# Residuals written over the raw weight piece: 8 raw slots and 4 high buffers in place of 6, 3 and 3

## The chip, the cores and the metric

The kernel runs on one core of a Trainium2 chip. The metric is the device time of one execution in microseconds (us). Engine names are those of the profile: PE (matrix products), ACT (scalar engine), DVE (vector engine), POOL (GpSimd), SP (the engine that issues most transfers). SPq, ACTq are their DMA-issuing instructions. PEclk is the share of TensorE's full clock that was granted.

## What is computed

Two transformer blocks on 256 tokens of width 1024, in float32. Cut to what matters here:

```
# first block
proj = rmsnorm(x) @ w_in                      # 1024 x 3584
x = x + concat(stick_breaking(...), group_norm(retention(...)) * silu(r_g)) @ w_out
hn = rmsnorm(x); x = x + moe(hn)              # router, top 4 of 32 experts, 1024x2048 and 1024x1024 each
x = x + (p @ w_ple_proj) * sigmoid(rmsnorm(x) @ w_ple_gate)
# second block
q, k, v, z, xbc, dt, gates = split(rmsnorm(x) @ w_in_2)
attn = gqa_attention(rope(norm(q)), rope(norm(k)), v) @ w_attn_proj_2
ssd = ssd_branch(z, silu(conv(xbc)), dt) @ w_ssd_proj_2
x = x + rmsnorm((g_attn * attn + g_ssd * ssd) @ w_out_2)
x = x + rmsnorm((silu(gate) * up) @ w_down_2)  # gate, up = rmsnorm(x) @ w_gate_up_2
```

## The kernel before

**Pieces.** All weights but the experts' are cut into 89 pieces of at most 128 x 2048 floats (1 MB), numbered in the order of use: 0 to 13 `w_in`, 14 to 17 `w_out`, 18 router, then the experts, then the late pieces 19 to 22 `ple_gate`, 23 `ple_proj`, 24 and 25 `q`, 26 `kv`, 27 `dt`, 28 to 33 `xbc`, 34 to 41 `gates`, 42 to 45 `z`, 46 and 47 `attn_proj`, 48 to 51 `ssd_proj`, 52 to 55 `out2`, 56 to 77 the feed-forward's `gate` and `up`, 78 to 88 its `ffn_down`.

**A piece's way.** SP loads it into a raw slot (L380). ACT copies it, rounded, into a high buffer (`split`, L1058, 1.9 us), when the piece has landed and the high buffer's previous piece was used. POOL subtracts the high part from the raw piece and writes the residual (L1888, four instructions a piece). PE makes each product as three matmuls: high by high, high by low, low by high (L467 to L469), and counts `w_used` up. A product waits for `w_low`, the count of finished POOL pieces.

**The ring** has 12 slots of 2048 columns. In the dense parts 6 hold raw pieces (piece n in slot n % 6), 3 high parts, 3 low parts. A raw slot may be loaded again once POOL has finished its piece (`w_low`). In the expert phase all 12 slots hold one chunk each of an expert's weights: 8 `up` chunks, 4 `down` chunks; `EXPERT_SLOT` gives chunk j its slot.

**Order.** Every engine runs a list written out by hand and waits in it. SP: x, pieces 0 to 2, positions and 14 small broadcasts, the first pieces up to `RAW`, then the constants (`consts_late`, 1.9 MB, L394), then the rest. ACT: `split_to(n)` makes all splits up to piece n at that place of its list; between them stand its evacuations of PSUM, exponentials and the first half of each norm. In most places the call is `split_to(x + 3)`, followed by a wait until PE has used piece x and by the evacuation of x. After the experts ACT first splits `BUF` late pieces, then begins the norm (L1062, L1072) of the ple part. DVE does norms, rotations, softmax maxima, the convolution and the SSD weights. POOL has the residuals alone. Before the late pieces POOL waits until all experts are done.

```
def load(key):
    n = number[key]
    if n >= RAW:
        sp.wait_ge(sem("w_low"), n - RAW + 1)
    fetch(key)
...
    if m >= BUF:
        act.wait_ge(sem("w_used"), place[keys[m - BUF]] + 1)
    split(m)
```

Of the kernel before, what the change touches and what calls it, by code (L numbers as in the profile page):

```python
# [13 lines left out]
F32 = mybir.dt.float32  # L14
# [25 lines left out]
EPS = 1e-6  # L40
SLOT = 2048
RING = 12
RAW = 6
BUF = 3
EXPERT_SLOT = (1, 2, 3, 4, 5, 0, 6, 7, 8, 9, 10, 11)
PER_EXPERT = 12
CONVK = 5
CC = 12
# [77 lines left out]
def build_program(nc, a, out):  # L126
# [5 lines left out]
    pieces, number = [], {}  # L132
# [17 lines left out]
    before_experts = len(pieces)  # L150
    ROUNDS = E + (PASSES - 1) * E
    base_c = before_experts + PER_EXPERT * ROUNDS
    late = len(pieces)
# [20 lines left out]
    place = {k: n if n < late else n - late + base_c for k, n in number.items()}  # L174
    keys = sorted(number, key=number.get)

    def raw_slot(key):
        return number[key] % RAW

# [6 lines left out]
    def slot_fills(s):  # L186

        return sum(1 for k in keys if number[k] < late and raw_slot(k) == s) if s < RAW else 0

    with ExitStack() as ctx:  # L190
# [5 lines left out]
        def sem(name):  # L196
            return sems[name]
# [29 lines left out]
        arena_byte, ring_byte = nc.lookup_mloc(arena).addr, nc.lookup_mloc(ring).addr  # L227
# [17 lines left out]
        def parts_at(name, byte, cols):  # L245

            return nc.alloc_sbuf_tensor_at(name, [P, cols], F32R, offset=byte)[:, :]
# [70 lines left out]


        HIGH = [parts_at(f"w_high{i}", ring_byte + 4 * SLOT * (RAW + i), SLOT) for i in range(BUF)]  # L320
        LOW = [parts_at(f"w_low{i}", ring_byte + 4 * SLOT * (RAW + BUF + i), SLOT) for i in range(BUF)]

        def slot(s):
            return ring[:, s * SLOT:(s + 1) * SLOT]
# [5 lines left out]
        def split_view(key):  # L330

            _, chunks, width = pieces[number[key]]
            return [x[number[key] % BUF][:, 0:chunks * width].rearrange("p (k n) -> p k n", k=chunks) for x in (HIGH, LOW)]

        def chain(eng, name):

# [33 lines left out]
        def _(sp):  # L370
            def load(key):
                n = number[key]
                if n >= RAW:
                    sp.wait_ge(sem("w_low"), n - RAW + 1)
                fetch(key)

            def fetch(key):
# [11 lines left out]
            for at, name in GAINS:  # L389
                n = a[name].shape[1]  # L390
# [7 lines left out]
            def expert_load(e, j):  # L398
                dst = slot(EXPERT_SLOT[j])
                if j < KC:  # L400
# [11 lines left out]

            for j, s in enumerate(EXPERT_SLOT):
                if s < RAW:
                    sp.wait_ge(sem("w_low"), max(n for n in range(late) if n % RAW == s) + 1)
                else:
                    sp.wait_ge(sem("w_used"), before_experts)
                expert_load(0, j)
# [25 lines left out]
            with sp.Else():  # L444
                for j, s in enumerate(EXPERT_SLOT):

# [582 lines left out]
        def _(act):  # L1029
# [16 lines left out]
            def split_to(n):  # L1046

                while done_splits[0] <= min(n, len(keys) - 1):
                    m = done_splits[0]
# [3 lines that stand above are left out]
# [826 lines left out]
        @block.gpsimd  # L1879
        def _(pool):  # L1880
            for m, key in enumerate(keys):
                if m == late:
                    pool.wait_ge(sem("w_used"), before_experts + PER_EXPERT * ROUNDS)
                pool.wait_ge(sem("w_high"), m + 1)
                quarter = size(key) // 4
                for part in range(4):
                    at = slice(part * quarter, (part + 1) * quarter)
                    ins = nc.gpsimd.tensor_tensor(LOW[m % BUF][:, at], slot(raw_slot(key))[:, at], HIGH[m % BUF][:, at].bitcast(F32),  # L1888
                                                  ALU.subtract)
                ins.then_inc(sem("w_low"), 1)  # L1890

# [26 lines left out]
```

## Time and profile before

| | us |
|---|---|
| median of 3 runs | 1757.93 (1756.92 to 1758.99) |
| the profiled execution | 1748.9 |
| its span, first to last instruction | 1747.1 |
| busy: PE, DVE, ACT, POOL | 1498.8, 510.3, 423.6, 472.6 |

The profiled execution was 9.0 us shorter than the median of the runs. Parts by time, as the timeline shows them: input products, stick-breaking and retention until 208 us, router until 239, experts until 1189, ple until 1245, input products of the second block until 1301, attention until 1400, SSD until 1468, output products until 1545, feed-forward until the end.

### The profile page before, as it was taken

The numbers are of one execution on the slowest core, as the hardware profiler recorded it, in microseconds if no ns is written. First come the engines' busy times: TensorE is split into PE (matmuls) and PEld (weight loads), VectorE is DVE, ScalarE is ACT, GpSimd is POOL, SyncE is SP. The second block draws the span as 40 slices with busy tenths as digits, with TensorE's granted clock in tenths as the row PEclk, the third lists the DMA queues.
The fourth block names the chain that finished last, engine by engine and source line by source line (L and its number), as shares of the span: only waits on it lengthen the run. The fifth ranks groups of instructions, "written<-read, shape, count | busy, mean of one in ns | idle before, by whom it ended". The sixth has DMA issues, their size and how long they took to land.

```text
span 1747.1 us, 19158 instructions
## 1 busy us (share of the span) xinstructions
PE 1498.8 (86%) x7437; PEld 848.9 (49%) x7438; DVE 510.3 (29%) x826; ACT 423.6 (24%) x503; POOL 472.6 (27%) x360
## 2 busy tenths in 40 slices
PE   6787689999888888989888888987876988989997
PEld 5565443333232332323232332325675766779986
DVE  1766611211121111111121111112396168231211
ACT  4553300110010101001010101004442734343332
POOL 5862100000000000000000000005592643668894
PEclk9988879999999999999999999999997999999999
DMA  8522459999999999999999999996452322445540
GB/s 297 178 76 73 155 238 416 418 415 419 416 417 417 416 418 416 417 416 418 416 417 417 416 418 416 418 415 232 132 182 64 121 82 68 148 145 180 182 169 24
DMA packets 135830, 502.32 MB, mean 288 GB/s; under 512 B 11948, under 2 KB 42148, under 8 KB 102852
## 3 DMA queue, kind: packets, MB, share of 16 engines
q1 hardware_dynamic: 134480, 499.00, 72.9%
q10 hardware_dynamic: 1267, 2.09, 0.4%
q8 instruction: 67, 1.10, 0.3%
q14 instruction: 16, 0.12, 0.0%
HBM read 500.01 MB, written 1.05 MB: 287 GB/s over the span
## 4 chain that ended last, share of the span: by engine, by line
PE 41%; DMA 21%; SPq 16%; DVE 14%; issue 4%; ACT 3%; POOL 0%; ACTq 0%; DVEq 0%
DMA ring<-in_w_up_gate 19%; SPq L405 14%; PE PS L467 7%; PE PS L716 7%; PE PS L468 7%; PE PS L469 7%; PE PS L734 6%; ACT w_high L1058 1%; DMA ring<-in_w_ple_gate 1%; SPq L380 1%; PE PS L688 1%; DMA cst<-consts 1%; DVE arena L1605 1%; DVE arena L1608 1%; DVE arena L1603 1%
## 5 line engine op out<-in xcount | busy, mean ns | idle before, releaser
L1888 POOL TENSOR_TENSOR w_low<-ring,w_high 128x512 fp32r<-128x512 f32 (+1 forms) x356 | 472.4, 1360 | 1254.4 <-PEq L817 1006.9
L716 PE MATMUL PS<-ring,arena 128*64 128x512 f32 x2048 | 475.0, 604 | 53.9 <-DMA ring<-in_w_up_gate 53.8
L716 PEld LDWEIGHTS PS<-ring,arena 128*64 128x64 f32 x2048 | 134.4, 137 | 378.2 <-issue 214.5
L734 PE MATMUL PS<-ring,arena 128*64 128x512 f32 x1024 | 226.8, 594 | 23.5 <-issue 23.5
L1058 ACT ACTIVATE w_high<-ring 128x2048 fp32r<-128x2048 f32 (+1 forms) x89 | 167.4, 1882 | 275.1 <-PE PS L469 252.8
L1168 ACT ACTIVATE arena<-arena 128x512 f32<-128x512 f32 x32 | 20.1, 630 | 811.2 <-DVE arena L1602 811.2
L1602 DVE TENSOR_SCALAR arena<-PS 128x512 f32<-128x512 f32 x32 | 22.1, 692 | 514.0 <-PE PS L716 514.0
L467 PE MATMUL PS<-w_high,XNT_h 128*128 128x512 f32 (+1 forms) x336 | 137.5, 409 | 21.6 <-DVE XNT_l L1345 8.6
L734 PEld LDWEIGHTS PS<-ring,arena 128*64 128x64 f32 x1024 | 84.6, 137 | 145.1 <-issue 145.1
L467 PE MATMUL PS<-XNT_h,w_high 128*128 128x256 f32 (+1 forms) x464 | 131.2, 283 | 4.1 <-DVE XNT_l L1345 3.5
L468 PE MATMUL PS<-w_low,XNT_h 128*128 128x512 f32 (+1 forms) x336 | 133.6, 398 | 0.0
L469 PE MATMUL PS<-w_high,XNT_l 128*128 128x512 f32 (+1 forms) x336 | 133.5, 397 | 0.0
L468 PE MATMUL PS<-XNT_l,w_high 128*128 128x256 f32 (+1 forms) x464 | 131.7, 284 | 0.0
L469 PE MATMUL PS<-XNT_h,w_low 128*128 128x256 f32 (+1 forms) x464 | 131.6, 284 | 0.0
L1611 DVE COPY arena<-PS 128x512 f32<-128x512 f32 x32 | 22.1, 692 | 266.2 <-PE PS L734 266.2
L467 PEld LDWEIGHTS PS<-XNT_h,w_high 128*128 128x128 f32 (+1 forms) x464 | 87.0, 188 | 5.5 <-issue 4.2
L469 PEld LDWEIGHTS PS<-XNT_h,w_low 128*128 128x128 f32 (+1 forms) x464 | 86.1, 186 | 0.3
L468 PEld LDWEIGHTS PS<-XNT_l,w_high 128*128 128x128 f32 (+1 forms) x464 | 86.0, 185 | 0.3
L467 PEld LDWEIGHTS PS<-w_high,XNT_h 128*128 128x128 f32 x336 | 65.1, 194 | 42.3 <-issue 12.3
L469 PEld LDWEIGHTS PS<-w_high,XNT_l 128*128 128x128 f32 x336 | 64.7, 193 | 15.2
L468 PEld LDWEIGHTS PS<-w_low,XNT_h 128*128 128x128 f32 x336 | 64.9, 193 | 14.7 <-issue 0.7
L741 PE MATMUL PS<-arena 64*128 64x512 f32 x264 | 65.6, 615 | 0.0
(316 smaller groups left out, 1486.4 us busy)
## 6 DMA issues: line engine op xcount, KB each, us to landing
ring<-in_w_up_gate SPq DMA_DIRECT2D x256, 1024.0 KB, 21.2
ring<-in_w_down SPq DMA_DIRECT2D x139, 1024.0 KB, 24.2
ring<-in_w_in SPq DMA_DIRECT2D x35, 1024.0 KB, 5.4
ring<-in_w_gate_up SPq DMA_DIRECT2D x22, 1024.0 KB, 5.1
ring<-in_w_out SPq DMA_DIRECT2D x8, 1024.0 KB, 5.1
ring<-in_w_ple_gate SPq DMA_DIRECT2D x4, 1024.0 KB, 17.7
ring<-in_w_ssd_proj SPq DMA_DIRECT2D x4, 1024.0 KB, 5.0
ring<-in_w_attn_proj SPq DMA_DIRECT2D x2, 1024.0 KB, 5.5
```

The lines of the kernel that those rows point to most:

```text
L405: sp.dma_start(dst, src).then_inc(landed[EXPERT_SLOT[j]], 16)
L467: nc.tensor.matmul(out, lhs[0], rhs[0], start=start, stop=False)
L468: nc.tensor.matmul(out, lhs[0], rhs[1], start=False, stop=False)
L469: return nc.tensor.matmul(out, lhs[1], rhs[0], start=False, stop=stop)
L716: ins = nc.tensor.matmul(PS[64 * (n % 2):64 * (n % 2) + 64, 4 + n // 2, :], x, w[:, n * 512:(n + 1) * 512], start=False, stop=c == KC - 1, ...
L734: ins = nc.tensor.matmul(PS[64 * n:64 * n + 64, 7, :], lhs, w[:, k, n * 512:(n + 1) * 512], start=c == 0, stop=c == KC - 1)
L741: ins = nc.tensor.matmul(PS[:, 2 * tb + n, :], SPT[64 * n:64 * n + 64, tb * P:(tb + 1) * P], YS[64 * n:64 * n + 64, :], start=False, stop= ...
L1058: nc.scalar.activation(HIGH[m % BUF][:, 0:size(key)], slot(raw_slot(key))[:, 0:size(key)], ACT.Copy).then_inc(sem("w_high"), 1)
L1168: nc.scalar.activation(SIG, GLU, ACT.Sigmoid, scale=1.702).then_inc(sem(sig_out), 1)
L1602: ts(GLU, PS[:, 4, :], 7.0, None, ALU.min).then_inc(sem("glu"), 1)
L1611: V.tensor_copy(YS, PS[:, 7, :]).then_inc(sem("y_slots"), 1)
L1888: ins = nc.gpsimd.tensor_tensor(LOW[m % BUF][:, at], slot(raw_slot(key))[:, at], HIGH[m % BUF][:, at].bitcast(F32), ALU.subtract)
```

## The change

Six raw slots become eight and three high buffers four. The three low buffers go: POOL writes the residual in place, over the raw piece. So a raw slot is free only when PE has used its piece, and SP waits for `w_used` of piece n - 8, not for `w_low` of piece n - 6. `split(m)` waits for PE's use of piece m - 4, not m - 3. POOL's wait for the end of the experts is gone. The calls of `split_to` keep their arguments. `EXPERT_SLOT` is changed so that the first late pieces follow the last expert's chunks into the same slots.

```diff
-RAW = 6
-BUF = 3
-EXPERT_SLOT = (1, 2, 3, 4, 5, 0, 6, 7, 8, 9, 10, 11)
+RAW = 8
+BUF = 4
+EXPERT_SLOT = (3, 4, 5, 6, 7, 0, 1, 2, 8, 9, 10, 11)
...
-        LOW = [parts_at(f"w_low{i}", ring_byte + 4 * SLOT * (RAW + BUF + i), SLOT) for i in range(BUF)]
+        LOW = [parts_at(f"w_low{i}", ring_byte + 4 * SLOT * i, SLOT) for i in range(RAW)]
...
                 if n >= RAW:
-                    sp.wait_ge(sem("w_low"), n - RAW + 1)
+                    sp.wait_ge(sem("w_used"), place[keys[n - RAW]] + 1)
...
                 if s < RAW:
-                    sp.wait_ge(sem("w_low"), max(n for n in range(late) if n % RAW == s) + 1)
+                    sp.wait_ge(sem("w_used"), max(n for n in range(late) if n % RAW == s) + 1)
...
             for m, key in enumerate(keys):
-                if m == late:
-                    pool.wait_ge(sem("w_used"), before_experts + PER_EXPERT * ROUNDS)
                 pool.wait_ge(sem("w_high"), m + 1)
...
-                    ins = nc.gpsimd.tensor_tensor(LOW[m % BUF][:, at], slot(raw_slot(key))[:, at], HIGH[m % BUF][:, at].bitcast(F32),
+                    ins = nc.gpsimd.tensor_tensor(LOW[raw_slot(key)][:, at], slot(raw_slot(key))[:, at], HIGH[m % BUF][:, at].bitcast(F32),
```

SP's list at the start, between the last broadcasts and the `w_out` pieces; `cst<-consts` is the 1.9 MB of constants, `ring<-in_w_in` a piece:

```order
 L391 DMA bc<-in_a_log_b 128x16
 L391 DMA bc<-in_d_skip 128x16
-L380 DMA ring<-in_w_in 128x4x512 x3
+L380 DMA ring<-in_w_in 128x4x512 x5
 L394 DMA cst<-consts 128x3810
-L380 DMA ring<-in_w_in 128x4x512 x8
+L380 DMA ring<-in_w_in 128x4x512 x6
 L380 DMA ring<-in_w_out 128x4x512 x4
```

Two pieces more, 6 and 7, stand ahead of the constants.

ACT's list at the end of the experts, in the branch that runs here and up to the end of the branches; each row is one split:

```order
-L1058 ACTIVATE w_high_66<-ring 128x2048
-L1058 ACTIVATE w_high_67<-ring 128x2048
-L1058 ACTIVATE w_high_65<-ring 128x2048
+L1058 ACTIVATE w_high_68<-ring 128x2048
+L1058 ACTIVATE w_high_65<-ring 128x2048
+L1058 ACTIVATE w_high_66<-ring 128x2048
+L1058 ACTIVATE w_high_67<-ring 128x2048
```

The split of piece 22 moved from behind the ple norm to ahead of it.

## Rows read from the trace of the kernel before

**Rows 1.** The chain of waits, whole run: shares of the span by line.

```profile
by line: DMA ring<-in_w_up_gate 18.8%; SPq L405 14.1%; PE PS L467 7.4%; PE PS L716 7.4%; PE PS L468 7.2%; PE PS L469 7.2%; PE PS L734 5.8%; issue 4.3%; ACT w_high L1058 1.0%; DMA ring<-in_w_ple_gate 1.0%; SPq L380 1.0%; PE PS L688 0.9%; DMA
```

**Rows 2.** Stretches: us, busy PE, PEld, DVE, ACT, POOL, PEclk, DMA share, GB/s.

```profile
371.00:1189.00 818.00, 719.47 (x3252) 253.20 (x3248) 135.55 (x283) 77.62 (x108) 0.00 (x0) 1.00 1.02 416
...
1264.00:1310.00 46.00, 36.32 (x299) 35.56 (x296) 43.76 (x36) 22.17 (x25) 45.16 (x32) 0.95 0.58 183
...
1545.00:1747.00 202.00, 191.32 (x1332) 178.45 (x1330) 32.93 (x48) 72.50 (x59) 157.48 (x124) 0.97 0.41 136
```

**Rows 3.** Chain of waits, its longest pieces: start, us, what.

```profile
24.77 15.67 DMA cst<-consts
47.92 1.91 ACT w_high L1058
49.89 6.71 POOL w_low L1888 x4
...
112.99 1.91 ACT w_high L1058
```

**Rows 4.** DMA rate in 40 slices of 18 to 45 us.

```profile
GB/s 132 229 189 124 42 29 95 121 236 323 331 328 338 356 358 337 416 401 446 475 441 411 434 434 386 390 391 357 406 392 400 367 376 388 388 388 385 388 388 388
```

**Rows 5.** Timeline after the experts, ACT and DVE: start, us, instruction, [idle before <-releaser].

```profile
1193.50 1.91 ACT L1058 ACTIVATE w_high<-ring 128x2048 fp32r<-128x2048 f32 x1 [0.80 <-DMA ring<-in_w_ple_gate]
...
1191.96 2.35 DVE L1656 TENSOR_TENSOR arena<-arena,PS 128x1024 f32<-128x1024 f32 x2 [1.48 <-PEq L818]
```

**Rows 6.** Timeline at the end of ple, ACT and DVE.

```profile
1227.39 1.92 ACT L1058 ACTIVATE w_high<-ring 128x2048 fp32r<-128x2048 f32 x1 [3.70 <-PE PS L469]
...
1232.54 1.22 DVE L1667 TENSOR_TENSOR arena<-arena,PS 128x1024 f32<-128x1024 f32 x1 [13.70 <-ACT arena L1216]
```

**Rows 7.** Timeline at the kv product, ACT and DVE.

```profile
1262.20 1.92 ACT L1058 ACTIVATE w_high<-ring 128x2048 fp32r<-128x2048 f32 x1 [2.87 <-PE PS L469]
...
1264.83 1.99 DVE L1353 TENSOR_TENSOR arena<-arena 128x1280 f32<-128x1280 f32 x1 [17.64 <-ACT arena L1227]
```

**Rows 8.** Timeline of the rotations on DVE, and of POOL beside them.

```profile
1281.91 1.30 DVE L1374 TENSOR_TENSOR arena<-arena 128x160 f32<-128x160 f32 x1
1283.24 0.32 DVE L1375 TENSOR_TENSOR arena<-arena 128x160 f32<-128x160 f32 x1
...
1283.67 26.35 POOL L1888 TENSOR_TENSOR w_low<-ring,w_high 128x512 fp32r<-128x512 f32 x20 [0.65 <-ACT w_high L1058]
```

**Rows 9.** Waits from 1190 to 1550 us: us in total, times, longest.

```profile
PE PS L877 <- DVE arena L1715: 9.5, 1, 9.5
...
PE PS L467 <- ACT arena L1268: 3.3, 3, 1.5
...
PE PS L960 <- DVE arena L1779: 2.7, 2, 2.1
...
PE PS L467 <- ACT arena L1283: 1.3, 1, 1.3
...
PE PS L467 <- POOL w_low L1888: 0.7, 1, 0.7
```

**Rows 10.** Timeline of ACT at the first SSD units.

```profile
1414.27 1.91 ACT L1058 ACTIVATE w_high<-ring 128x2048 fp32r<-128x2048 f32 x1 [7.76 <-PE PS L469]
1416.09 0.58 ACT L1279 ACTIVATE arena<-PS 128x512 f32<-128x512 f32 x1
```

**Rows 11.** Timeline of PE in the SSD loop, the fifth unit.

```profile
1448.76 3.68 PE L960 MATMUL PS<-arena 128*128 128x64 f32 x16 [2.06 <-DVE arena L1779]
```

**Rows 12.** Timeline of DVE in the SSD loop, POOL busy and POOL idle.

```profile
1428.79 2.94 DVE L1769 TENSOR_TENSOR arena<-arena 128x256 f32<-128x256 f32 x2
...
1463.60 0.75 DVE L1769 TENSOR_TENSOR arena<-arena 128x256 f32<-128x256 f32 x2
```

**Rows 13.** Timeline of DVE after the out2 product, POOL busy and POOL idle.

```profile
1537.87 2.16 DVE L1861 TENSOR_TENSOR arena<-arena 128x1024 f32<-128x1024 f32 x1
...
1541.46 1.22 DVE L1861 TENSOR_TENSOR arena<-arena 128x1024 f32<-128x1024 f32 x1
```

More of the change, by code:

```diff
@@ L332, in split_view @@
             _, chunks, width = pieces[number[key]]
-            return [x[number[key] % BUF][:, 0:chunks * width].rearrange("p (k n) -> p k n", k=chunks) for x in (HIGH, LOW)]
+            return [x[:, 0:chunks * width].rearrange("p (k n) -> p k n", k=chunks) for x in (HIGH[number[key] % BUF], LOW[raw_slot(key)])]
         def chain(eng, name):
```

## The prediction

> **What bounds the kernel now.** I read the chain of waits first, then busy time by stretch, the list of waits, and the timelines at the places the diff touches. The chain's largest part is the experts' weights: transfers of `w_up_gate` 18.8% and their issue at L405 14.1% [rows 1]. From 371 to 1189 us the transfers run without a pause at 416 GB/s [rows 2]. Nothing in the diff makes these 403 MB fewer or faster; what moves the expert phase's start moves its end by as much. The feed-forward is bound by PE, 191.3 us busy of 202 [rows 2]. What is left for the change are the stretches ahead of, between and behind these two. There the ring is not the limit that its depth suggests: in the dense parts from 1190 to 1550 us PE waits for a residual once, for 0.7 us [rows 9]. What costs there is the place of a split in ACT's list. The change therefore has to be judged by waits that move on ACT, by transfers that move on SP, and by what POOL's work does to DVE.
>
> **The start, a cost.** SP now queues pieces 6 and 7 ahead of the constants. The constants are on the chain: issued at 24.77 they land 15.67 us later, at 40.4, with DVE waiting; DVE's angles release ACT, ACT's split at 47.92 releases POOL at 49.89, and its four instructions release PE at 56.6 [rows 3]. Transfers of the queue are served in order there, at 388 GB/s [rows 4], so 2 x 1.05 MB ahead cost 2.10 / 0.388 = 5.4 us. The bounds are 0 (if ACT, POOL or PE had another reason to be late; the chain shows none) and 5.4. I take 5.4. This work and all behind it is a chain up to the experts, whose 12 chunks are fetched long before PE wants them in both kernels, so nothing later absorbs it. Five chunks instead of six now wait for the router product: no effect, they still land before PE comes.
>
> **The early part, a small gain.** `split(m)` no longer waits for PE's use of m - 3. The one early split on the chain that this frees takes 1.91 us at 112.99 [rows 3]; behind it stands an exponential that waits for DVE anyway. Between 0 and 1.9; I take 0.5.
>
> **The end of the experts, a cost.** ACT now makes four splits before the ple norm. In the kernel before the third begins at 1193.50, as soon as its piece lands, 0.80 us after the second ended (so pieces land 1.91 + 0.80 = 2.7 us apart), and ends at 1195.4, 1.1 us after x2 is ready at 1194.3 [rows 5]. ACT is the last there. The fourth piece lands 2.7 us after the third and is split until 1198.0: +2.6. Bounds 1.9 (already landed) and 5. POOL's dropped wait buys nothing: its residuals are done well before XNT.
>
> **The late splits, gains.** At each `split_to(x + 3)` the split of x + 3 waited for the use of x, and the evacuation of x stood behind it. With four buffers it waits for x - 1 and is over when x is used. That takes 1.9 us, and the table load behind it (1.3 us where there is one), off the way from product to evacuation. What it is worth depends on what is late next.
> - *ple.* The split at 1227.39 stands ahead of the sigmoid, and DVE's L1667 starts at 1232.54 [rows 6]. At most 1.9 + 1.3 = 3.2; PE's first half of `ple_proj` (until about 1230.2) and its second (1233.0) come next: 2.5.
> - *kv and rotations.* The split at 1262.20 delays the kv evacuation and with it DVE, which starts at 1264.83 [rows 7]. DVE is then the chain until PE's wait of 9.5 us at L877 [rows 9]: 43.8 us busy of 46 [rows 2]. A start 1.8 us earlier passes on. POOL is busy in the same stretch, 45.2 of 46 us, and while it is, a rotation step takes 1.30 us against 0.32 in a gap of POOL [rows 8]. POOL's last passes end at 1310.0 and should end some 2 us earlier, but its one gap may close. Between 0.5 and 4: 2.0.
> - *Attention.* PE waits three times for ACT's sigmoid L1268, 3.3 us [rows 9], each with a split and a table load ahead of it. 2.5 of these go, and 0.6 at the attention's end: 3.1.
> - *SSD.* ACT's exponential of the second unit starts at 1416.09, behind a split that waited 7.76 us [rows 10], though PE had its input ready at 1408.6. So DVE's weights are late, and PE waits 2.7 us for L1779 and 1.3 for L1283 [rows 9]. In the slow stretch behind the longest of these PE needs 3.68 us for 16 small matmuls [rows 11], against about 1.9 elsewhere in the loop. All this together 4 to 7; against it stands POOL's pass of piece 49, which moves from behind the loop to its last unit, where DVE's scaling would take 2.94 instead of 0.75 us [rows 12]. 5.0, between 0 and 7.
> - *After ssd_proj and out2.* POOL's pass is over before DVE's residual adds, which take 2.16 us beside POOL and 1.22 without it [rows 13]; two such on the chain: 1.9.
>
> **Sum.** +5.4 - 0.5 + 2.6 - 2.5 - 2.0 - 3.1 - 5.0 - 1.9 = -7.0 us. The profiled execution took 1748.9, so 1741.9 of its kind; it lies 9.0 below the median of the runs, to which the forecast refers: 1757.9 - 7.0 = 1750.9.
>
> **In place or not.** POOL's instructions keep their shape, inputs and number; only the address written differs. I cost that at nothing. If writing over the input cost each pass something, POOL has cover of 0.6 us a piece at 5.0 us a piece in the feed-forward's down part, and beyond it PE would wait there; that is inside the lower chance below.
>
> **Rival 1, slower: POOL's passes collide with DVE.** The earlier passes move into DVE's chains. Its place is the SSD loop and the rotations: a unit whose scaling and weights run beside POOL costs 2.94 - 0.75 = 2.2 us more for the scaling [rows 12] and about 1.6 for the weights. If two units on the path pay 3.8 each, SSD gives back 7.6 against its 5.0; the rotations keep the end they have; the residual adds gain nothing. 5.4 + 2.6 - 2.5 - 3.1 + 2.6 = +5.0: 1762.9. It decides once more than one unit's collision is on PE's path. For it: DVE has no slack in the last units. Against it: in the middle of the loop DVE idles between units, so a collision there is hidden.
> The Trainium skill, "SBUF — State Buffer", section "Who interferes with whom", says that a DVE instruction with two SBUF inputs and a GpSimd instruction that reads SBUF exclude each other, whoever starts first. By that rule the collision moves with POOL's pass as in this rival, and the trace's 1.30 against 0.32 us agrees; which of the two lists is then late, the rule doesn't say.
>
> **Rival 2, no change.** PE or DVE are next in most places and the late gains come out at half, 7 us, against 8.0 of cost: 1758.
>
> **Rival 3, faster by more: the start delay is hidden.** If the constants' delay doesn't reach PE in full, the cost at the start goes from 5.4 to about 1: 1746.5. Against it is the unbroken chain of rows 3.
>
> **Chances.** Forecast 0.55, rival 3 0.14, rival 2 0.18, rival 1 0.13. A measurement of this kernel can tell about 0.2%, 3.5 us, from no change. Faster by over 0.2% 0.69, within 0.2% 0.18, slower 0.13. The range from 1743 to 1760 takes in the bounds of the SSD term downwards and rival 2 upwards; rival 1's end is left out.
>
> **What would show it.** The constants' landing at 45.9 instead of 40.4, and PE's first wait for a residual 5.4 us longer; the first expert matmul about 5 us later; four splits ahead of the ple norm, and its table load at 1195.4 + 2.6 + 4.9; no wait of PE at L1268 and L1283 and one or none at L960; L1861 at 1.2 us twice. Wrong would be: a first expert matmul that is not later (rival 3), or DVE's L1769 and L1778 beside POOL right ahead of PE waits in the last SSD units (rival 1).

## The result, and the profile after

The changed kernel takes 1742.1 us (median of 6 runs, 1738.3 to 1746.0); the kernel before, on the same chip, 1755.4 (6 runs, 1750.7 to 1759.0). The ratio is 0.9925, 95% interval 0.9902 to 0.9948: faster by some 13 us, with 9 to 17 in the interval. The profiled execution took 1738.3 us with a span of 1736.5, against 1748.9 and 1747.1 before: 10.6 us less. The forecast was 1750.9 with a range from 1743 to 1760: the direction was right, the time below the range.

I set the two traces side by side at marks on TensorE that both have. "Later" is after against before; a term is what a stretch adds to that.

| mark on PE | before | after | later | term | forecast |
|---|---|---|---|---|---|
| resumes behind the constants | 56.65 | 61.73 | +5.1 | +5.1 | +5.4 |
| first expert's L758 | 230.36 | 233.54 | +3.2 | -1.9 | -0.5 |
| last expert's L741 ends | 1191.68 | 1194.60 | +2.9 | -0.3 | 0 |
| ple's norm, L476 | 1199.86 | 1205.28 | +5.4 | +2.5 | +2.6 |
| third norm, L476 | 1240.66 | 1244.08 | +3.4 | -2.0 | -2.5 |
| rotations done, L877 | 1310.58 | 1310.80 | +0.2 | -3.2 | -2.0 |
| SSD begins, L950 | 1403.24 | 1399.46 | -3.8 | -4.0 | -3.1 |
| ssd_proj begins | 1484.52 | 1477.87 | -6.7 | -2.9 | -5.0 |
| feed-forward begins | 1548.06 | 1537.46 | -10.6 | -3.9 | -1.9 |

Behind the last mark the difference stays at 10.6.

A second profile of each kernel (r_before and r_after, below) gives the same terms for the experts' end (+2.5), attention (-4.0), SSD (-2.9) and what lies behind ssd_proj (-4.0). Four terms come out differently: the start +3.5, the early part -0.5, ple -2.4, kv and rotations -1.3. In the last, 1.9 us are the product of q and kv, which ran at a lower clock in r_after (0.81 for 0.96 from 1245 to 1270 us); without that product the term is -3.2 in both pairs. The second pair's sum is -9.5.

**The start.** The chain of waits after, its pieces up to where PE resumes (start, us, what), answers to [rows 3]:

```profile
29.13 17.89 DMA cst<-consts
...
54.97 6.72 POOL w_low L1886 x4
61.73 0.79 PE PS L467
```

The timeline of DVE, first instruction that reads the constants, after:

```profile
47.12 0.17 DVE L1387 CAST stat<-pos_i 128x2 f32<-128x2 int32 x1 [26.52 <-DMA cst<-consts]
```

The request goes out at 29.13 instead of 24.77 and the constants land at 47.0 instead of 40.4. DVE then finds POOL idle: this CAST takes 0.17 us and the two instructions of L1389 behind it 0.52, where they took 0.69 and 1.50 beside a pass of POOL in the kernel before. That makes up 1.5 us, so PE is 5.1 us later, not 6.6.

**The end of the experts.** Timeline of ACT after, for [rows 5]:

```profile
1191.58 3.90 ACT L1058 ACTIVATE w_high<-ring 128x2048 fp32r<-128x2048 f32 x2 [7.40 <-PE PS L734]
1196.29 1.91 ACT L1058 ACTIVATE w_high<-ring 128x2048 fp32r<-128x2048 f32 x1 [0.81 <-DMA ring<-in_w_ple_gate]
1198.92 1.91 ACT L1058 ACTIVATE w_high<-ring 128x2048 fp32r<-128x2048 f32 x1 [0.73 <-DMA ring<-in_w_ple_gate]
1200.85 1.28 ACT L1062 ACT_TABLE_LOAD   x1
```

Four splits, the last 0.73 + 1.91 = 2.64 us behind the third, and the norm's table load stands behind it.

**The late stages.** List of waits after, from 1190 to 1550 us, for [rows 9] (who waits for whom: us in total, times, longest):

```profile
PE PS L877 <- DVE arena L1715: 7.4, 1, 7.4
PE PS L960 <- DVE arena L1779: 4.4, 2, 3.6
PE PS L950 <- DVE arena L1758: 2.8, 1, 2.8
...
PE PS L467 <- POOL w_low L1886: 1.3, 1, 1.3
```

PE's waits for L1268 (3.3 us) and L1283 (1.3) are gone. The one for L1715 is 2.1 shorter. The one for L1779 has grown, and a new one for POOL has come, at the start of `ssd_proj`, where PE waited 2.2 us for the low half of the norm before. In the same stretch ACT's splits waited for a use by PE 30 times and 122.6 us before, now 10 times and 37.3 us: the change does what it says.

The longer wait for L1779 lies in the last SSD unit. Timelines of POOL, DVE and PE there, after:

```profile
1451.99 5.75 POOL L1886 TENSOR_TENSOR w_low<-ring,w_high 128x512 fp32r<-128x512 f32 x4 [15.12 <-ACT w_high L1058]
...
1452.44 2.51 DVE L1769 TENSOR_TENSOR arena<-arena 128x256 f32<-128x256 f32 x2
1454.87 1.75 DVE L1778 TENSOR_TENSOR arena<-arena 128x512 f32<-128x512 f32 x1
1456.64 1.63 DVE L1779 TENSOR_TENSOR arena<-arena 128x512 f32<-128x512 f32 x1
...
1458.33 3.36 PE L960 MATMUL PS<-arena 128*128 128x64 f32 x16 [3.64 <-DVE arena L1779]
```

POOL's pass is that of piece 49, the only one behind the fourth unit; DVE's four instructions take 5.9 us where they take 0.75 + 0.69 + 0.69 = 2.1 beside an idle POOL. PE waits 3.64 us. Then the 16 small matmuls take 3.36 us, against 2.00 in the kernel before, and `attn_proj` begins at half the clock: the granted clock is 0.50 from 1461.5 to 1463 and 1.00 from 1466 on. In the kernel before it is 1.00 from the product's start.

Timeline of DVE after, the residual adds of [rows 13]:

```profile
1528.18 1.23 DVE L1861 TENSOR_TENSOR arena<-arena 128x1024 f32<-128x1024 f32 x1
...
1530.86 1.23 DVE L1861 TENSOR_TENSOR arena<-arena 128x1024 f32<-128x1024 f32 x1
```

### The profile page after: what moved, and what is told of

Read it like the earlier page. It is cut to its first block, busy times and chain, and to the rows that moved or that the text cites. A ratio compares the mean times of both kernels' runs of the same rounds, so it can differ in the third digit from the quotient of the medians.

```text
span 1736.5 us, 19164 instructions
## 1 busy us (share of the span) xinstructions
PE 1491.7 (86%) x7437; PEld 836.4 (48%) x7438; DVE 523.3 (30%) x826; ACT 422.3 (24%) x503; POOL 471.5 (27%) x360
## 4 chain that ended last, share of the span: by engine, by line
PE 42%; DMA 19%; SPq 16%; DVE 14%; issue 4%; ACT 3%; POOL 1%; ACTq 0%; DVEq 0%
DMA ring<-in_w_up_gate 18%; SPq L405 14%; PE PS L716 8%; PE PS L467 7%; PE PS L469 7%; PE PS L468 7%; PE PS L734 6%; SPq L380 1%; PE PS L688 1%; DMA cst<-consts 1%; DMA ring<-in_w_ple_gate 1%; DVE arena L1608 1%; DVE arena L1605 1%; DVE arena L1603 1%; PE PS L722 1%
## 5 line engine op out<-in xcount | busy, mean ns | idle before, releaser
L1886 POOL TENSOR_TENSOR w_low<-ring,w_high 128x512 fp32r<-128x512 f32 (+1 forms) x356 | 471.3, 1359 | 1239.2 <-ACT w_high L1058 1239.0
L716 PEld LDWEIGHTS PS<-ring,arena 128*64 128x64 f32 x2048 | 135.6, 137 | 372.3 <-issue 226.0
L734 PEld LDWEIGHTS PS<-ring,arena 128*64 128x64 f32 x1024 | 73.1, 137 | 161.1 <-issue 161.1
L469 PE MATMUL PS<-w_high,XNT_l 128*128 128x512 f32 (+1 forms) x336 | 132.7, 395 | 0.0
L469 PE MATMUL PS<-XNT_h,w_low 128*128 128x256 f32 (+1 forms) x464 | 131.7, 284 | 0.0
L469 PEld LDWEIGHTS PS<-XNT_h,w_low 128*128 128x128 f32 (+1 forms) x464 | 85.9, 185 | 0.3
L469 PEld LDWEIGHTS PS<-w_high,XNT_l 128*128 128x128 f32 x336 | 64.4, 192 | 15.1
L741 PE MATMUL PS<-arena 64*128 64x512 f32 x264 | 65.6, 615 | 0.0
## 6 DMA issues: line engine op xcount, KB each, us to landing
ring<-in_w_up_gate SPq DMA_DIRECT2D x256, 1024.0 KB, 20.9
```

The source lines that it names most:

```text
L469: return nc.tensor.matmul(out, lhs[1], rhs[0], start=False, stop=stop)
L716: ins = nc.tensor.matmul(PS[64 * (n % 2):64 * (n % 2) + 64, 4 + n // 2, :], x, w[:, n * 512:(n + 1) * 512], start=False, stop=c == KC - 1, ...
L734: ins = nc.tensor.matmul(PS[64 * n:64 * n + 64, 7, :], lhs, w[:, k, n * 512:(n + 1) * 512], start=c == 0, stop=c == KC - 1)
L741: ins = nc.tensor.matmul(PS[:, 2 * tb + n, :], SPT[64 * n:64 * n + 64, tb * P:(tb + 1) * P], YS[64 * n:64 * n + 64, :], start=False, stop= ...
L1886: ins = nc.gpsimd.tensor_tensor(LOW[raw_slot(key)][:, at], slot(raw_slot(key))[:, at], HIGH[m % BUF][:, at].bitcast(F32), ALU.subtract)
```

## The experiments

The theory to test: all of the gain comes from the fourth high buffer, by splits that need not wait for the piece in use; in place and the deeper ring bring nothing but the later constants. The rivals: the ring or the in-place write brings part of it; or TensorE's granted clock does. The medians, each with the ratio to the kernel before on its chip:

| kernel | us (runs) | ratio, 95% interval |
|---|---|---|
| e_consts6 | 1734.9 (4) | 0.9878, 0.985 to 0.9906 |
| e_wait3 | 1765.1 (10) | 1.0057, 1.0038 to 1.0076 |
| e_split3 | 1740.3 (4) | 0.9904, 0.9871 to 0.9937 |
| e_split49 | 1740.2 (4) | 0.9911, 0.9884 to 0.9937 |
| e_buf4 | 1734.5 (4) | 0.9873, 0.9839 to 0.9907 |
| e_raw9 | 1763.9 (1) | |
| e_poolset | 1717.5 (1) | |
| e_wait3_tail | 1753.2 (10) | 0.9975, 0.9952 to 0.9998 |
| e_parts8 | 1739.7 (4) | 0.9919, 0.9888 to 0.9949 |
| e_wait3_mid | 1745.6 (1) | |
| e_best | 1731.9 (6) | 0.9881, 0.9857 to 0.9905 |
| e_best8 | 1735.0 (6) | 0.9894, 0.9871 to 0.9917 |
| r_before | 1751.9 (1) | |
| r_after | 1742.6 (6) | 0.9923, 0.9899 to 0.9948 |
| r_buf4 | 1738.1 (6) | 0.9901, 0.9877 to 0.9925 |
| r_best | 1732.7 (6) | 0.988, 0.9855 to 0.9905 |

### The fourth buffer undone: e_wait3

```diff
-                        act.wait_ge(sem("w_used"), place[keys[m - BUF]] + 1)
+                        act.wait_ge(sem("w_used"), place[keys[m - (BUF - 1 if True else BUF)]] + 1)
```

> The changed kernel with four high buffers and eight raw slots as they are, but each split waits for the use of the piece three before it, as the three buffers made it do. Theory 1 (the fourth buffer, by the earlier splits that it allows, brings all the gains; the eight slots bring only the cost at the start): the stages behind ple lose their gains of 3.2 + 4.0 + 2.9 + 4.0 us and the early part its 2.2, so the end comes about 14 to 16 us later than with the change, 1757 to 1758 us, slower than or level with the kernel before (1755.4). Theory 2 (the low part in place and the deeper ring bring the gain): at most 3 us are lost, 1742 to 1745 us. Theory 3 (half and half: the later passes of POOL matter only where they met VectorE): about 1750 us.

1765.1 us, by the ratio 10 above the kernel before. From ple's norm to the feed-forward every mark lies 9.6 to 9.8 us behind the kernel before: L476 at 1209.47 (+9.6), L877 at 1320.16 (+9.6), L950 at 1412.95 (+9.7), the feed-forward at 1557.83 (+9.8). List of waits from 1190 to 1560 us:

```profile
PE PS L877 <- DVE arena L1715: 9.6, 1, 9.6
...
PE PS L467 <- ACT arena L1268: 3.3, 3, 1.5
PE PS L960 <- DVE arena L1779: 2.6, 2, 2.1
...
PE PS L467 <- ACT arena L1283: 1.3, 1, 1.3
```

These are the waits of [rows 9] again, to 0.1 us, though ring and place of the low parts are the changed kernel's. The ring of eight and the in-place write win nothing in the late stages. What is left above the kernel before are the costs at the start and at the experts' end: the first expert is 6.5 us late and the norm another 3.2. My expectation of 1757 to 1758 had the mechanism but not the size. It counted at most 16.3 us lost against the changed kernel; the profile shows 20.4. I had left out ple (2.0), and the early part and the experts lose 4.2 together instead of 2.2. The early part's gain is the buffer's too: with the strict wait the first expert is 3.3 us later than with the change, 0.7 of it already at the start.

### A longer ring without the buffer: e_raw9

```diff
-RAW = 8
-BUF = 4
+RAW = 9
+BUF = 3
```

> The changed kernel with nine raw slots and three high buffers, so the low parts in place and a longer ring, without the fourth buffer. One more piece of 4 x 512 columns then stands ahead of the constants. Theory 1 (a longer ring only costs the landing of the pieces ahead of the constants, some 2.7 us each): VectorE's wait for the constants rises from 26.5 to about 29 us, nothing else gains, the three splits ahead of ple's norm are as before, and the profiled time is about 1757 to 1760 us. Theory 2 (the ring brings a part of the gain): below 1750 us.

1763.9 us, one run. Timeline of DVE at the constants:

```profile
49.56 0.17 DVE L1387 CAST stat<-pos_i 128x2 f32<-128x2 int32 x1 [28.97 <-DMA cst<-consts]
```

The wait is 2.5 us longer than the change's and 8.8 longer than before's 20.2. No late stage gained. Three pieces more ahead of the constants make the first expert 7.9 us later than in the kernel before (238.23). The total is even 4 us above what I wrote: from L877 to the feed-forward PE takes 243.1 us against 237.5. Slower products are part of that, `ssd_proj` with 24.3 us for 22.7 among them (out2 is 1.3 faster), and so is a longer wait at L950 (5.3 us in two against 3.6). Why they come here isn't shown.

### The buffer without the rest: e_buf4

The kernel before with `RAW = 4`, `BUF = 4` and as many low buffers; nothing is written in place.

```diff
-RAW = 6
-BUF = 3
+RAW = 4
+BUF = 4
```

> The kernel before with four raw slots, four high buffers and four low ones (low parts not in place), so the fourth buffer alone, at the price of two raw slots. The constants are then requested two pieces earlier. Theory 1 (the fourth buffer brings all the gains; raw slots beyond four bring nothing once loads are waited on by POOL's pass): the stages from kv to out2 gain as with the change, 3.2 + 4.0 + 2.9 + 4.0 us, and the start is 3 to 5 us earlier than before, so 1735 us or less, faster than the change. Theory 2 (four slots are too few: the experts' first loads or the late pieces come too late): waits for landings at the start or behind the experts eat 5 us or more, 1745 to 1760 us.

1734.5 us, and 1738.1 in its repetition below. Its waits of PE at L877, L960 and L1848 behind the experts are those of the changed kernel to 0.1 us, and those for L1268 and L1283 are gone here too. The start's chain of waits:

```profile
19.43 18.52 DMA ring<-in_w_in
38.04 1.92 ACT w_high L1058
...
49.84 6.71 POOL w_low L1888 x4
56.60 0.79 PE PS L467
57.81 0.43 PE PS L469
...
61.31 0.23 PE PS L469
```

The constants now land 5 us before those of the kernel before (DVE's CAST at 35.4), yet PE resumes at 56.60, as there (56.65), where I had expected it 3 to 5 us earlier: piece 4, which now waits for a raw slot, has become the late one, with ACT's split at 38.04 and the evacuation behind it. So the start's delay can be undone, but more than that isn't to be had there. The chain also shows the two levels of TensorE's clock, 1.2 and 2.4 GHz: a matmul of L469 takes 0.43 us and, from 61 us on, 0.23.

### The constants back in their place: e_consts6

```diff
-            for key in keys[3:RAW]:
+            for key in keys[3:6]:
...
-            for key in keys[RAW:late]:
+            for key in keys[6:late]:
```

> The changed kernel with one thing undone: the late constants are requested behind piece 5 again, ahead of pieces 6 and 7. Theory 1 (the start costs what the two pieces take to land, and all of it reaches the end): VectorE's wait for the constants at its first read of cst falls from 26.5 back to about 20.2 us, TensorE resumes at about 56.6 us instead of 61.7, and the end comes 5 us earlier, 1737 us. Theory 2 (something later in the experts or in the early part absorbs a shift of the start): the wait falls as well, but the experts' end and the total stay within 1.5 us of the changed kernel, about 1742 us.

1734.9 us, 7 below the changed kernel, where I expected 5. Timeline of DVE:

```profile
41.76 0.66 DVE L1387 CAST stat<-pos_i 128x2 f32<-128x2 int32 x1 [21.02 <-DMA cst<-consts]
```

PE resumes at 57.85, 3.9 us earlier than in the changed kernel, the first expert is 3.5 earlier and the feed-forward 2.8. The start's cost reaches the end, as forecast: 2.8 us by this profile, in which the product of q and kv took 2.2 us more than in the changed kernel's, and 7 by the medians. Its size scatters: over the eight profiles that have the change's start (this kernel twice, and the experiments that leave it alone) DVE's CAST starts between 44.6 and 47.5 us and the first expert's L758 between 232.3 and 234.0, against 40.3 and 40.5, 230.1 and 230.4 in two profiles of the kernel before. The profile of the result had one of the latest CASTs.

### The splits by stage: e_wait3_tail and e_wait3_mid

As e_wait3, but the strict wait holds only from `ssd_proj`'s first piece on (e_wait3_tail), or only for kv, dt and xbc (e_wait3_mid):

```diff
+                        act.wait_ge(sem("w_used"), place[keys[m - (BUF - 1 if m >= number[("ssd_proj", 0, 0)] else BUF)]] + 1)
...
+                        act.wait_ge(sem("w_used"), place[keys[m - (BUF - 1 if number["kv"] <= m < number[("gates", 0, 0)]  else BUF)]] + 1)
```

> The changed kernel in which the splits from the first piece of ssd_proj on wait for the use of the piece three before, as with three buffers; all earlier splits stay free. It prices the fourth buffer behind the SSD. Theory 1 (what the change won behind ssd_proj's first product comes from these splits, since POOL is then done when VectorE reads the eviction in L1848 and L1861): L1848 takes 1.5 to 2.2 us again, out2 ends some 4 us later measured from the start of ssd_proj, total 1746 us. Theory 2 (it is the granted clock of TensorE, which the shorter pauses ahead keep up, and not the splits): out2 takes 22.7 us as with the change, total within 1.5 us of 1742 us.

1753.2 us: 11 above the changed kernel, where I expected 4. From L950 (1406.03 here, 6.6 late in this profile already) to the feed-forward (1552.75) PE takes 8.7 us more than with the change. List of waits from 1190 to 1560 us:

```profile
PE PS L950 <- DVE arena L1758: 5.5, 3, 2.8
...
PE PS L960 <- DVE arena L1779: 2.3, 2, 2.1
```

The waits inside the SSD units are back, because piece 48, whose split stands in the fourth unit, is already `ssd_proj`'s: it waits there for the use of piece 45, which is that unit's own z product, and what stands behind it on ACT is late for the next unit, with POOL's pass beside that. Then come L1848 and L1861 beside POOL and the slower out2 (23.3 us). The clock goes both ways here: `ssd_proj` takes 1.5 us more and out2 0.6, `attn_proj` 1.8 less. So theory 1 holds for the adds but the gain isn't only theirs: the splits from piece 48 on are worth 8.7 us, against 10.6 for the whole change with its costs, and 3.9 of them lie in the SSD units.

> The changed kernel in which only the splits of kv, dt and the six xbc pieces wait for the use of the piece three before. It prices the fourth buffer in the rotations. Theory 1 (those splits bring the 3.2 us that the change won between ple's end and L877): from TensorE's first transposition of the third norm to the first matmul of L877 takes 3 us more than the changed kernel's 66.7 us; what comes behind is shifted by the same. Theory 2 (the gain there comes from what the stage finds at its start: POOL is ahead already): the stretch takes 66.7 us within 1 us.

From the third norm to L877 71.5 us, 4.8 more than with the change. 1.6 of them are a slower product, as it also varies between two profiles of one kernel (168 matmuls in 27.35 us against 25.74); the other 3.2 are a wait for POOL (0.6), the longer gap and product around it (0.5), and 2.1 at L877, which waits 9.6 us as in [rows 9]. Without the slower product this is theory 1. It is one run.

### The fourth split ahead of ple's norm: e_split3

```diff
-                for m in range(late, late + BUF):
+                for m in range(late, late + BUF - 1):
...
-            done_splits[0] = late + BUF
+            done_splits[0] = late + BUF - 1
...
+            act.wait_ge(sem("w_used"), before_experts + PER_EXPERT * ROUNDS)
             split_to(number[("ple_proj")])
```

> The changed kernel with three of the four first late pieces split ahead of ple's norm, the fourth behind the norm's evacuation. Theory 1 (the fourth split stands on the path at the end of the experts, at its own 2.5 us): PE's first transposition of ple's norm comes 2.5 us earlier behind the experts' end, and the total is 1739.5 us. Theory 2 (the split is only moved into ple, where TensorE then waits for piece 22): the gain is given back by the end of ple's products, total 1742 us.

PE's norm comes 8.22 us behind the experts instead of 10.67, and the next norm is 2.2 us earlier too, so ple doesn't give it back. It goes in the product behind: 27.83 us against 25.74 for the same 168 matmuls. That this product is slow because of the edit isn't shown: it took 27.6 us in the changed kernel's second profile too. The total, 1740.3, can't be told from the changed kernel's.

### Piece 49's pass out of the last SSD unit: e_split49

```diff
-            split_to(number[("attn_proj", 0)] + 3)
             norm(4, "y_mul", Y, NY)
```

> The changed kernel with the split of piece 49 moved from ahead of the SSD norm to behind its squares, so that POOL's pass over it no longer lies beside VectorE's work on the last SSD unit. Theory 1 (that pass holds VectorE up: L1769, L1778 and L1779 of the last unit take 2.5, 1.75 and 1.6 us): TensorE's last wait for L1779 falls from 3.6 to under 1 us, and the end comes 2 to 3.5 us earlier, 1739 us. Theory 2 (the wait is the unit's own chain; nothing to do with POOL): the wait stays over 3 us, total 1742 us. Theory 3 (the pass is late for ssd_proj instead): the wait goes, one of 2 to 4 us for w_low comes at the start of ssd_proj, total 1742 to 1744 us.

Timeline of DVE in the last unit (L1768 is L1769 of the other kernels, and so on, since a line is gone):

```profile
1452.46 0.75 DVE L1768 TENSOR_TENSOR arena<-arena 128x256 f32<-128x256 f32 x2
1453.13 0.69 DVE L1777 TENSOR_TENSOR arena<-arena 128x512 f32<-128x512 f32 x1
1453.85 0.69 DVE L1778 TENSOR_TENSOR arena<-arena 128x512 f32<-128x512 f32 x1
```

5.9 us have become 2.1, and the 3.64 us of waiting are gone. `attn_proj` behind it takes 11.49 us instead of 13.32: PE doesn't pause, and its granted clock is 1.00 from the start of the product. At its end 6.9 us are won (L476 at 1467.72 against 1474.61). Then 1.9 are lost to a longer wait ahead of `ssd_proj` (3.2 us for the norm's low half, against 1.35 for POOL): the moved split now stands with that of piece 50 ahead of the norm's evacuation. Another 1.3 are lost in `ssd_proj`, 24.03 us against 22.72. 3.7 are left at the feed-forward. The timed median shows 1.9, within the scatter of either.

### What POOL costs VectorE: e_poolset and e_parts8

e_poolset writes zeros for the low parts of pieces 28 to 36 (their differences are left out); e_parts8 does the whole work in half as large instructions.

```diff
+                    if number["dt"] < m <= number[("xbc", 5)] + 3:
+                        ins = nc.gpsimd.memset(LOW[raw_slot(key)][:, at].bitcast(F32), 0.0)
+                        continue
...
+                parts = 8 if number["dt"] < m <= number[("xbc", 5)] + 3 else 4
```

> The changed kernel in which POOL writes zeros over the raw pieces 28 to 36 instead of the differences (the low parts of these nine pieces are left out), so that it reads nothing from SBUF while VectorE does the rotations. It prices POOL's passes beside VectorE. Theory 1 (VectorE's instructions of 1.3 us for what takes 0.32 us alone are held up by POOL's passes over the same SBUF): L1353 to L1715 of the rotations run at 0.3 to 0.7 us, TensorE's wait for L1715 (7.4 us) is gone, and the profiled time falls 8 to 20 us below 1738. Theory 2 (their time is the instructions' own): VectorE's durations and the wait stay within 1 us.

Timelines of POOL and DVE where they meet, and the only wait of PE from 1250 to 1335 us:

```profile
1282.94 1.93 POOL L1887 MEMSET w_low<- 128x512 f32 x4 [5.88 <-ACT w_high L1058]
...
1283.56 0.33 DVE L1373 TENSOR_TENSOR arena<-arena,cst 128x160 f32<-128x160 f32 x1
...
PE PS L895 <- DVE arena L1730: 1.4, 1, 1.4
```

All 24 rotation steps take 0.32 to 0.33 us, where 22 of them took 1.2 to 1.3. Seven of the 24 ran beside a MEMSET, which reads nothing, the others beside an idle POOL. PE's waits of 7.4 (L877) and 14.5 us (L895) shrink to 1.4, and L895 comes at 1307.54 instead of 1328.09. The run, a single one, took 1717.5 us: POOL's passes over these nine pieces cost this kernel some 20 us, more than the whole change brought. A MEMSET of 128x512 also takes 0.5 us where the subtraction takes 1.3, so POOL is busy for less than half as long; the 20 us price the passes as they are, not the shared reading alone.

> The changed kernel with POOL's pass over the pieces 28 to 36 cut into eight instructions of 128x256 instead of four of 128x512; the same work. Theory 1 (each of VectorE's 24 short instructions in the rotations waits for the end of the POOL instruction under way, 1.30 us against 0.33 us with nothing read by POOL): they fall to 0.6 to 0.8 us, the rotations end 10 to 14 us earlier, TensorE's wait for L1715 (7.4 us) goes, and the total is 6 to 14 us below 1742 us, less what POOL's own overhead of more instructions costs. Theory 2 (the two engines share the port by turns of a fixed time, whatever the instruction's size): VectorE's durations stay at 1.3 us, total 1742 us or more.

Timelines of DVE and POOL and the wait of PE:

```profile
1281.62 0.74 DVE L1372 TENSOR_TENSOR arena<-arena,cst 128x160 f32<-128x160 f32 x1
1311.40 6.98 DVE L1687 SCALAR_TENSOR_TENSOR arena<-arena,vecT 128x256 f32<-128x256 f32 x8
...
1276.71 45.45 POOL L1887 TENSOR_TENSOR w_low<-ring,w_high 128x256 fp32r<-128x256 f32 x56 [2.46 <-ACT w_high L1058]
...
PE PS L895 <- DVE arena L1730: 20.9, 1, 20.9
```

and the convolution of the changed kernel, behind POOL's last pass:

```profile
1311.21 3.25 DVE L1687 SCALAR_TENSOR_TENSOR arena<-arena,vecT 128x256 f32<-128x256 f32 x8
```

With POOL instructions of 128x256 a rotation step takes 0.74 us instead of 1.30: its time follows the length of the POOL instruction beside it (0.82 and 1.37 us there), as if VectorE waited for the one under way, and not for turns of a fixed time. The Trainium skill, "SBUF — State Buffer", section "Who interferes with whom", states that a VectorE instruction with two SBUF inputs contends with a GpSimd instruction that reads SBUF and not with one that only writes it. The trace agrees in both halves: 0.74 and 1.30 us beside the subtractions, 0.33 beside the MEMSET. The wait at L877 is gone, as I expected, but the total is 2 us below the changed kernel's and not 6 to 14, and can't be told from it. But a piece takes POOL 45.45 / 7 = 6.5 us instead of 5.3, so its passes reach into the convolution, whose eight steps take 6.98 us instead of 3.25. The wait for L895 grows by 6.4 us to 20.9. The 7.4 us won at one wait were lost at the next: from the third norm to L895 PE takes 83.7 us (2.0 of them a slower product of q and kv) and 84.0 with the change. By these figures the smaller instructions are worth some 2 us at most.

### Together: e_best, e_best8 and the repetitions

e_best is e_buf4 with three splits ahead of ple's norm and piece 49's split moved; e_best8 adds the smaller POOL instructions.

> The kernel before with four raw slots, four high and four low buffers, the split of piece 49 behind the squares of the SSD norm, and three splits ahead of ple's norm instead of four. The parts measured alone against the kernel before: 23 us for the first (1734.5), about 2 for the second, about 2 for the third. Theory 1 (they add up as far as TensorE's granted clock lets them): 1730 to 1733 us. Theory 2 (the clock takes the later two back, as it did with three splits alone, whose shorter pause was followed by slower products): 1734.5 us within 1 us.

> The same, with POOL's pass over the pieces 28 to 36 in eight instructions each. Theory 1 (VectorE waits for the POOL instruction under way): 6 to 14 us below the kernel without it, 1718 to 1727 us. Theory 2 (it waits turns of a fixed time): the same as without, 1731 to 1735 us.

1731.9 us, as the first theory had it, and 1735.0 with the smaller instructions, where I expected 1718 to 1727: they bring nothing here either. L895 comes 0.7 us earlier (1323.16 against 1323.86), and then `ssd_proj` takes 25.5 us against 24.1 and out2 24.3 against 22.7.

> The kernel before once more, unchanged, for a second profile. Theory 1 (the durations of the products are the clock's, and differ between two runs of one kernel): out2's product of 96 matmuls takes 22.7 or 24.2 us, not the 24.6 us of the first profile, in one of the four products behind the SSD or ple at least 1 us differs, and the span lies anywhere from 1747 to 1758 us. Theory 2 (they belong to the schedule): each product and each wait is within 0.3 us of the first profile's.

> The changed kernel once more, unchanged, timed in five rounds. Theory 1 (clock): the product of q, kv and dt (168 matmuls) takes 25.7 or 27.9 us, those of attn_proj 11.5 to 13.4 us, out2's 22.7 or 24.2 us, each independent of the first profile; the waits agree within 0.2 us. Ratio to the kernel before 0.990 to 0.995. Theory 2 (schedule): every product within 0.3 us of the first profile.

> The kernel with four raw slots, four high and four low buffers once more, timed beside the changed kernel on the same chip. It should be 5 to 8 us below the changed kernel (the start's cost undone and more), 1734 to 1736 us.

> The same with three splits ahead of ple's norm and the split of piece 49 behind the squares, once more, beside the other two on the same chip. Theory 1: 2 to 4 us below the one without these two edits. Theory 2 (the clock takes them back): within 1 us of it.

Both theories on the clock hold, each in other places; that out2 would change in the kernel before was wrong. The times of PE's products, in us:

| product | before | r_before | e_wait3 | after | r_after |
|---|---|---|---|---|---|
| ple, first 48 | 11.5 | 13.5 | 11.5 | 11.5 | 13.2 |
| q, kv (168) | 25.7 | 25.7 | 25.7 | 25.7 | 27.6 |
| attn_proj (48) | 11.5 | 11.5 | 11.5 | 13.3 | 13.4 |
| out2 (96) | 24.6 | 24.6 | 24.6 | 22.7 | 22.7 |

The stretch from 1205 to 1217 us, the transpositions of ple's norm and the first part of the product behind them, in the changed kernel and in its second profile (us, busy PE, PEld, DVE, ACT, POOL, PEclk, DMA share, GB/s):

```profile
1205.00:1217.00 12.00, 11.07 (x48) 9.18 (x49) 5.05 (x11) 4.76 (x10) 9.24 (x7) 0.81 0.18 59
...
1205.00:1217.00 12.00, 10.68 (x39) 8.83 (x40) 5.29 (x11) 3.77 (x11) 9.60 (x8) 0.64 0.17 63
```

ple's product and that of q and kv differ by 1.7 to 2.1 us between two runs of one kernel, at clocks of 0.81 and 0.64 here: that is scatter, and most of the 4 us by which the second profile's last mark lies later. attn_proj and out2 repeat to 0.1 us within these two kernels: they go with the schedule. (In e_buf4 and its repetition attn_proj took 12.8 and 13.4.) The strict wait loses 1.9 us in out2 and the change as much in attn_proj, behind its pause of 3.64 us. In out2 the granted clock was 0.92 before (1513 to 1537 us) and 1.00 after (1505 to 1528). For out2 that isn't certain of every schedule with the buffer: ten of the thirteen profiles that have it show 22.7 us, three (e_split3, e_poolset, e_best8) 24.3.

Timed side by side, the changed kernel takes 1742.6 us, the one with the buffer alone 1738.1, the one with all three edits 1732.7. Its runs (1729.3 to 1738.8) lie almost wholly below the changed kernel's (1738.6 to 1744.3): it beats both kernels of this case. The buffer alone is 4.6 us below the changed kernel, just short of the 5 to 8 that I expected. How the 5 us between r_buf4 and r_best divide over the two small edits wasn't settled, and not that they are that much: in the earlier runs, on two chips, the ratios to the kernel before were 0.9873 without them and 0.9881 with them, no gain.

## Why the prediction was right or wrong

**What held.** That the gain is in the dense stages behind the experts and that the experts' stream only passes a shift on (416 and 417 GB/s, and a clock of 1.00 before and after). The start's cost, 5.1 for 5.4, a size with luck in it: the constants landed 6.6 us later and VectorE made up 1.5, and in the second pair of profiles the cost is 3.5. The fourth split at the experts' end, 2.5 for 2.6. ple, 2.0 for 2.5. In place at no cost: POOL's instruction takes 1359 ns in the mean, 1360 before.

**What failed.** 8.8 us lie between the forecast and the time. 2.5 of them are the level: I set the change against a median of three runs, 1757.9, and the same kernel's median over six was 1755.4. The larger part, 6.3, is the change itself, -13.3 for -7.0; by the profiles it is 3.6. The terms of the sum that were mis-sized:
- *The early part*, 0.5 forecast and 1.9 measured, but 0.5 in the second pair: the miss of this term isn't certain. I looked for splits on the chain and found one. But the rotations of the early part are DVE chains with POOL beside them as well, and PE's wait for L1338 there went from 11.8 to 10.5 us, and to 10.3 in the second pair, where a longer wait for L1446 (11.6 against 10.6) took it back.
- *kv and rotations*, 2.0 forecast, 3.2 measured, and 3.2 by e_wait3_mid without its slower product. The earlier start passed on as I said; I gave nothing for POOL's wait of 0.7 us and the gap around it, though [rows 9] has that wait.
- *Attention*, 3.1 forecast, 4.0 measured: all 3.3 us of waits for L1268 went, I counted 2.5 of them. Of the rest, 0.4 is a shorter wait at L950, the SSD's start.
- *SSD*, 5.0 forecast, 2.9 measured. Here rival 1's mechanism came true in one unit: I had costed DVE's scaling for it (0.75 to 2.94 us) but not what it does to PE. It is a pause of 3.64 us and then 1.4 us of slower matmuls in L960 and 1.8 in attn_proj. The sign that I had written down for this rival, L1769 and L1778 beside POOL right ahead of a wait of PE, showed. Without that pass in the last unit (e_split49) the same stretch gains 6.9 us more up to `attn_proj`'s end. The rival's condition, more than one unit on PE's path, wasn't met.
- *Behind ssd_proj*, 1.9 forecast, 3.9 measured. The two adds that run without POOL gave what I said. The other 1.9 is out2, 22.7 us for 24.6, at a granted clock of 1.00 for 0.92, and it repeats in the second profile of either kernel: a term of the clock that stands in no line of my sum.

So the sum failed at its terms, not at its mechanism. The surest misses, alike in both pairs of profiles, are the clock of out2 (1.9, put at nothing), kv and rotations without their product (1.2), attention (0.9) and, the other way, SSD (2.1). In the first pair four gains were too small and one clearly too large. I took the middle of most bounds, where the waits in [rows 9] could all have been counted in full; the range was too narrow as well: with every term that had bounds at its better end the sum is 12.2 us lower than the forecast, 1738.7, and the range stopped 7.9 below it. Rival 3 (the start hidden) gave 1746.5 and fell: the delay reached the end, and e_consts6 took it back. Rival 2 fell with the late gains. A better reading of the diff was there to be had: by the terms of the sum the costs (5.4 and 2.6) come from RAW and from the fourth early split, and the gains from the fourth buffer alone.

The difference of some 3 us between the timed gain and the profiled one is not explained by any stage; the runs of one kernel differ by 6 to 11 us, and two profiles of each kernel don't average that out.

## What to carry to other kernels

When one edit changes two depths at once, split the sum by depth: here one more output buffer was worth some 20 us (e_wait3 against the change), and two more input slots cost 3 to 7 (e_consts6), because a transfer that others waited for was queued behind the pieces that fill them. Before a helper engine's pass is moved earlier, look whose instructions it will lie beside. Here an instruction of 0.3 us took about as long as the helper's instruction beside it. Taking the helper's subtractions away, and with them the residuals, won 20 us; smaller helper instructions won little or nothing, since they moved the cost to the next stage. Put no small gain of an edit against one run: the same products differed by 2 us between two profiles of one kernel, with the granted clock.

## What the runs showed of the hardware

- VectorE's 128x160 instructions with two SBUF inputs took 1.30 us beside POOL instructions of 128x512, 0.74 beside those of 128x256, and 0.33 beside a MEMSET or an idle POOL (e_parts8, e_poolset). POOL itself was hardly held up: 1.32 us an instruction on average beside VectorE, 1.25 without.
- A pause of PE of 3.6 us, 16 small matmuls ahead of a product of 48, was followed by 12.4 to 13.4 us for the product in all nine profiles that had the pause, 11.5 in the nine without. In the changed kernel the granted clock was 0.50 at its start (1461.5 to 1463 us) and 1.00 from 1466 us on; in the kernel before it was 1.00 throughout.
- Halving POOL's instructions raised its time for one piece from 5.3 to 6.5 us: 0.81 us for 128x256 beside VectorE, against 1.32 for twice the columns.
